# Two transformer blocks on one core: another order of output slabs, a later norm, and a third joint pair of neighbourhood scores

## The chip, the cores and the metric

The kernel runs on one core of one Trainium2 chip. The metric is the device time of one execution in microseconds, and the time of a version is the median over its runs. Engines are named as the profile names them: PE is the matrix engine (PEld its weight loads), DVE the vector engine, ACT the scalar engine, POOL GpSimd and SP the engine that issues the weight transfers.

## What is computed

The input is one sequence of 256 tokens with 1024 features. A first model of two layers is followed by a second of four. The change touches the two layers of the first model only. One of its layers is, cut to what matters:

```
proj = rms_norm(x) @ w_in[l]                 # split into the inputs of four mixers, four heads each
a_out = neighbourhood_attention(...)         # NA: scores + a bias table
b_out = diff_attention(...)                  # two softmaxes per head, subtracted
b_out = rms_norm(b_out, diff_subln[l]) * (1 - lambda_init)     # norm over each head's 64 features
c_out = gqa_attention(...)
d_out = mla_attention(...)
mix = concatenate([a_out, b_out, c_out, d_out]) @ w_o[l]       # 1024 x 1024
x = x + rms_norm(mix, post_mix_norm[l])
x = x + rms_norm(swiglu(rms_norm(x, pre_ffn_norm[l])), post_ffn_norm[l])
```

## The kernel before

All weights stream from memory in units of 128 x 2048 numbers (1 MB). SP loads a unit into one of three `raw` buffers. ACT rounds it to `whi` (L840, `act_hi`), DVE forms the rest `wlo = raw - whi` (L849, `dve_lo`), and each product is done as three matmuls, `hi*hi`, `lo*hi` and `hi*lo`. Every engine has its own instruction stream, written by hand, and runs it in order. Engines meet only in semaphores, on which an instruction waits until a count is reached.

The mixing stage of a layer is a table, `MIX`, of 38 slots (h = 0 to 37). In each slot PE does, in this order: its quarters of weight units; the transposes of one attention head's probabilities (L701, into `pso`), in the slot two after that head's scores; the scores of one head or of a joint pair (L715, into `psu`, and `psy` for the second of a pair); the product with the values of the head whose scores are three slots old (L730, into `psm`); and last, where the table says so, a "turn". Twenty items (heads) are worked on, one begun in each of the slots 12 to 31: four GQA (items 0 to 3), eight halves of the differential heads (4 to 11), four NA (12 to 15) and four MLA (16 to 19). DVE reads an item's scores, adds the table where there is one, and takes the maximum (L810 with a table, L804 without); ACT takes the exponential (L774) and copies the transposed probabilities (L760); DVE divides the finished head into its columns of `rows` (L785 to L796).

The output product runs while the last heads are still being computed. A **turn** m (0 to 7) takes 128 columns (two heads) of `rows`: PE transposes them (L584, two matmuls), ACT casts them into `ahi` (L617), DVE subtracts to get `alo` (L621) and counts the semaphore `m_lo`. A **slab** s (0 to 3) is one weight unit of `w_o` (unit 11 + s of the layer) and consumes the turns 2s and 2s + 1. It has four quarters of six matmuls each (L604, 128x512): two token tiles t, times two halves of its 256 rows. Slots 26 to 29 hold the quarters of slab 0, slots 30 to 33 those of slab 1, slots 34 and 35 two each of slab 2, slots 36 and 37 two each of slab 3. Slab results gather in the four banks of `psy` (tile 0 in banks 0 and 1, tile 1 in banks 2 and 3). The second score of a joint pair also uses bank 2, so slab 0 waits at its third quarter (slot 28) until DVE has read the last joint score.

The columns of `rows` stand in the order GQA, differential, NA, MLA. Turns 2 and 3 are thus those of the differential heads and wait for `mix_ready`, which DVE counts when the norm of these heads is applied. The norm has three steps: `sub_sums` on DVE in slot 26 (L1358 to L1361), a square root on ACT in slot 27 (L1268), `sub_norm` on DVE in slot 27 (L1365 to L1369). The square root and the exponential have different function tables on ACT, so an ACT_TABLE_LOAD stands before the root, another after it (L856), and one more in slot 33, ahead of the root of the next norm.

Of the kernel before, what the change touches and what calls it, by code (L numbers as in the profile page):

```python
# [9 lines left out]
D = 1024  # L10
# [3 lines left out]
HD = 64  # L14
# [31 lines left out]
class Plan:  # L46
# [30 lines left out]
    def value(self, h):  # L77
# [1 line left out]


MIX = Plan([2 if u is None else 4 for u in W_IN1], [3, 3, 2] + [2] * 11 + [1] * 20 + [2] * 4, range(12, 32),
           [17, 19, 28, 29, 30, 31, 33, 35], "00 01 10 02 03 11 12 13",
           [2, 3, 5, 7, 10, 11, 13, 14, 18, 22, 26, 30, 34], 24)
FOX = Plan([4] * 13, [3, 4, 1] + [2] * 30, [9, 10, 11, 12, 13, 14, 15, 16, 17, 18, 19, 20, 23, 24, 25, 26],
           [14, 16, 18, 20, 26, 27, 28, 30], "00 01 10 11 02 12 03 13", None, 23)
SWA = Plan([4] * 6, [2] * 8 + [1] * 15 + [2, 2, 1, 2, 2], range(6, 22), [11, 13, 15, 17, 20, 21, 23, 25],
# [23 lines left out]
def build(nc, wts, ada, ada_b, x_in, c_row, rel_bias, col1, row1, gain_mix, gain_ffn, col2, row2,  # L110
# [4 lines left out]
    with ctx:  # L115
# [18 lines left out]
        rows = sb("rows", [P, NT, D])  # L134
# [449 lines left out]
                last = nc.tensor.transpose(psu[:, bank, t * P:(t + 1) * P], rows[:, t, m * P:(m + 1) * P], ident[:])  # L584
            last.then_inc(m_tr, 1)

        def pe_slab_quarter(pe, l, c, s, part, g, first_t=0):


            t = first_t if part < 2 else 1 - first_t  # L590
            if part == 0:
                pe.wait_ge(lo_done, unit_no(l, c + s) + 1)
            if part < 2:
                pe.wait_ge(m_lo, 8 * g + 2 * s + part + 1)
            k = part_of(c + s)
            toks = slice(t * P, t * P + P)
            if s == 3 and part >= 2:
                chunks = [(0, part - 2), (1, part - 2)]
            else:
                chunks = [(part % 2, 0), (part % 2, 1)]  # L600
            for ff, half in chunks:
                cols = slice(ff * 1024 + half * 512, ff * 1024 + half * 512 + 512)
                for j, (h, b) in enumerate(((ahi, whi[:, k]), (alo, whi[:, k]), (ahi, wlo[:, k]))):
                    last = mm(psy[:, 2 * t + half, :], h[:, (2 * s + ff) % 4, toks], b[:, cols],  # L604
                              start=(s == 0 and ff == 0 and j == 0), stop=(s == 3 and ff == 1 and j == 2),
                              skip_group_check=True)
                if s == 3 and ff == 1 and 2 * t + half < 3:
                    last.then_inc(y_ready, 1)
            if part == 3:
                last.then_inc(unit_mm, 1)  # L610
# [131 lines left out]
        def pe_mix1_turn(pe, l, I0, h):  # L742


            m = MIX.turn.get(h)
            if m is not None:
                if m in (2, 3):
                    pe.wait_ge(mix_ready, l + 1)
                else:
                    pe.wait_ge(o_evac, I0 + (2 * m + 2 if m < 2 else 2 * m + 6))  # L750
                pe_turn(pe, l, m)

        def act_copy(act, I0, items, plan, h):
# [100 lines left out]
        def act_table(func):  # L854

            nc.scalar.activation(spare[:], epsc[:], func)  # L856
# [220 lines left out]
        def na_table(h):  # L1077
            return lambda t: fold(nab[:], NT, 4, SEQ)[:, t, h]
# [11 lines left out]
        def heads1(l):  # L1090
            out, b0 = [], l * 32
            for c in range(2):
                for kv in range(2):
                    ps = slice(64 * kv, 64 * kv + 64)
                    out.append(item(gqT[ps, c * SEQ:(c + 1) * SEQ], gkT[ps, :],
                                    [gv[:, kc * P + kv * HD:kc * P + (kv + 1) * HD] for kc in range(2)],
                                    (2 * c + kv) * HD, pre=(gqa_ready, l + 1), vpre=(bank_free, b0 + 4)))
            for h in range(4):
                for which in range(2):
                    p0, c = 64 * (h % 2) + 32 * which, (h // 2) * SEQ  # L1100
                    ps = slice(p0, p0 + 32)
                    out.append(item(dfq[ps, c:c + SEQ], dfk[ps, c:c + SEQ],
                                    [dfv[:, kc * 256 + h * HD:kc * 256 + (h + 1) * HD] for kc in range(2)],
                                    256 + h * HD, table=distance_table, slope=2.0 ** (-8.0 * (h + 1) / 4), pair=which,
                                    pre=(bank_free, b0 + 6), vpre=(bank_free, b0 + 7)))
            for h in range(4):
                ps, c = slice(64 * (h % 2), 64 * (h % 2) + 64), (h // 2) * SEQ
                out.append(item(naq[ps, c:c + SEQ], nak[ps, c:c + SEQ],
                                [nav[:, kc * 256 + h * HD:kc * 256 + (h + 1) * HD] for kc in range(2)],
                                512 + h * HD, table=na_table(h), tpre=(na_ready, l + 1),  # L1110
                                pre=(bank_free, b0 + 9), vpre=(bank_free, b0 + 10)))
            for h in range(4):
                out.append(item(qcT[0:96, h * SEQ:(h + 1) * SEQ], kcT[0:96, h * SEQ:(h + 1) * SEQ],
                                [mv[:, kc * 256 + h * HD:kc * 256 + (h + 1) * HD] for kc in range(2)],
                                768 + h * HD, pre=(ml_cev, 4 * l + 4), vpre=(ml_evac, l + 1)))
            return out

        def pe_mix1(pe, l):
# [18 lines left out]
            def quarter(j, part):  # L1137
# [3 lines left out]
                if j >= 11:  # L1141
                    if j == 11 and part in (0, 2):
                        pe.wait_ge(bank_free, b0 + 10)
                        if part == 2:
                            pe.wait_ge(max_ready, I0 + sum(MIX.joint))
                        pe.wait_ge(ml_cev, 4 * l + 4)
                    pe_slab_quarter(pe, l, 11, j - 11, part, l)
                    return
                u, at = W_IN1[j], j - (j > C1_SMALL)
                if u == 9:  # L1150
# [44 lines left out]
        def act_mix1(act, l):  # L1195
# [27 lines left out]
            for h in range(MIX.slots):  # L1223
# [38 lines left out]
                if h in (17, 18, 19, 20):  # L1262
                    act.wait_ge(ml_ctr, 4 * l + h - 16)
                    to, h0 = qcT if h < 19 else kcT, (h - 17) % 2 * 2
                    nc.scalar.copy(to[0:96, h0 * SEQ:(h0 + 2) * SEQ], psy[0:96, 3]).then_inc(ml_cev, 1)
                if h == 27:
                    act.wait_ge(sub_sum, l + 1)
                    nc.scalar.activation(gs[:, 1, 0:8], gs[:, 0, 0:8], ACT.Sqrt, bias=epsc[:], scale=1.0 / HD).then_inc(sub_std, 1)  # L1268
                    act_table(ACT.Exp)
                if h in MIX.turn:  # L1270
                    act_turn(act, l, C1_O, MIX.turn[h], l)
                if h == 33:
                    act_table(ACT.Sqrt)
                if j is not None and j < 14:
                    act_hi(act, l, j + SPLIT)

        def dve_mix1(dve, l):
# [71 lines left out]
                nc.vector.tensor_copy(fold(kcat, NT, 4, 96)[:, :, :, 64:96],  # L1349
                                      kr.unsqueeze(2).to_broadcast([P, NT, 4, 32])).then_inc(ml_rope, 1)  # L1350

            dh = rows[:, :, 256:512]
            dh4 = dh.rearrange("p t (h d) -> p t h d", h=4)
            sq, gain64 = qf[:, 0:512], qf[:, 512:512 + HD]

# [14 lines left out]
                                        ALU.mult).then_inc(mix_ready, 1)  # L1370

            for h in range(MIX.slots):
                dve_steps(dve, I0, items, MIX, h, l)
                if h == 3:
                    latent_norm()
# [9 lines left out]
                    head_rope()  # L1385
                if h == 15:
                    latent_rope()
                if h == 26:
                    sub_sums()
                if h == 27:  # L1390
                    sub_norm()
                if h in MIX.lo:
                    dve_lo(dve, l, MIX.lo[h] + SPLIT)
                if h in (16, 20):
# [690 lines left out]
def _weights(a):  # L2085
    units = []
    for l in range(DEPTH1):
# [5 lines left out]
        small[:, :768] = a["mla_w_uq"][l].reshape(2, P, 384).transpose(1, 0, 2).reshape(P, 768)  # L2093
        small[:, 768:1280] = a["mla_w_ukv"][l]
        units += [small if u is None else columns[u] for u in W_IN1]
        w_o = a["w_o"][l].reshape(4, 256, D)[[2, 1, 0, 3]]
        w_o[0] = w_o[0].reshape(4, HD, D)[[0, 2, 1, 3]].reshape(256, D)
        units += _slabs(w_o.reshape(D, D)) + _ffn_units(a["ffn_w_gate_up"][l], a["ffn_w_down"][l])
    seen = {"swa": 0, "gla": 0, "fox": 0}
# [93 lines left out]
```

## Time and profile before

| what | value |
|---|---|
| median of 3 runs (lowest to highest) | 1984.73 us (1979.16 to 1984.73) |
| profiled execution: time / span | 1984.8 us / 1983.0 us |
| PE busy | 1896.8 us, 96% of the span |
| DVE busy / ACT busy | 68% / 50% |
| mixing stage of layer 0, slot 28 begins / slot 34 begins | 126.02 us / 151.28 us |
| mean granted clock of PE | 0.984 |

A row of the timeline gives start, duration, engine, line, operation, the tile written and the tiles read, the number of instructions, and in brackets how long the engine had sat idle before it and what released it. PE's matmuls overlap, so the step from one start to the next is what a matmul costs, not its duration. Layer 1 of the first model repeats layer 0's rows some 344.3 us later (its turn 2 starts at 476.92 us, that of layer 0 at 132.62 us).

### The profile page before, as it was taken

To read this page: it belongs to the slowest core of one execution; us is meant where nothing else is said; L and a number is where in the kernel's file an instruction comes from. 1 tells how busy PE (TensorE), PEld (TensorE's weight loads), DVE (VectorE), ACT (ScalarE), POOL (GpSimd) and SP (SyncE) were. 2 spreads that over 40 slices of the span, in tenths; PEclk is the share of its full clock that TensorE was granted. 3 is DMA by queue.
4 is the path that set the end of the run, shared out by engine and by line. 5 is a ranking of instruction groups with operands and counts; after the bars stand their busy time and mean duration, and the time that the engine had idled before them with its cause. 6 is when DMAs were issued, how large, how long until landed. Compare 5 with 4: busy or idle time off the path is not lost. (4 is left out here: it accounts for less than half of the span.)

```text
span 1983.0 us, 34544 instructions
## 1 busy us (share of the span) xinstructions
PE 1896.8 (96%) x13474; PEld 1741.4 (88%) x13474; DVE 1341.8 (68%) x2132; ACT 996.3 (50%) x1533; POOL 92.8 (5%) x103
## 2 busy tenths in 40 slices
PE   7899999999999999999998999998999999999998
PEld 7788999888899987899978889997889998879997
DVE  4766888665788776688877578886446555665555
ACT  5766333766633366633374463336555334755333
POOL 3102000000000000000000000001800000000000
PEclk9899999999999999999999999999999999999999
DMA  8416988542688842588843258884334554324552
GB/s 290 168 69 196 360 317 317 202 149 77 232 317 310 313 175 80 214 322 313 315 180 118 99 225 324 310 316 175 136 131 165 190 190 169 128 86 170 191 188 87
DMA packets 60210, 412.21 MB, mean 208 GB/s; under 512 B 8576, under 2 KB 8768, under 8 KB 11344
## 3 DMA queue, kind: packets, MB, share of 16 engines
q1 hardware_dynamic: 55584, 401.33, 54.6%
q0 software_dynamic: 4528, 9.56, 1.8%
q8 instruction: 62, 1.02, 0.2%
q14 instruction: 36, 0.29, 0.0%
HBM read 409.71 MB, written 3.16 MB: 208 GB/s over the span
## 5 line engine op out<-in xcount | busy, mean ns | idle before, releaser
L840 ACT CAST whi<-raw 128x2048 fp32r<-128x2048 f32 x282 | 537.9, 1907 | 635.8 <-PE psu L499 424.1
L849 DVE TENSOR_TENSOR wlo<-raw,whi 128x2048 fp32r<-128x2048 f32 (+2 forms) x297 | 651.6, 2195 | 300.2 <-ACT whi L840 299.8
L499 PE MATMUL psu<-hhi,whi 128*128 128x256 f32 x1920 | 537.0, 280 | 0.0
L499 PE MATMUL psu<-hlo,whi 128*128 128x256 f32 x1920 | 536.0, 279 | 0.0
L499 PE MATMUL psu<-hhi,wlo 128*128 128x256 f32 x1920 | 535.8, 279 | 0.0
L499 PEld LDWEIGHTS psu<-hhi,whi 128*128 128x128 f32 x1920 | 360.8, 188 | 3.0
L499 PEld LDWEIGHTS psu<-hlo,whi 128*128 128x128 f32 x1920 | 360.8, 188 | 2.4
L499 PEld LDWEIGHTS psu<-hhi,wlo 128*128 128x128 f32 x1920 | 360.8, 188 | 0.0
L995 DVE CUSTOM_DVE_ANT_0 ada_raw<-ada_raw,cvec 128x1024 f32<-128x1024 f32 x192 | 226.8, 1219 | 0.6 <-DMA ada_raw<-ada 0.6
L655 PE MATMUL psy<-whi,ahi 128*128 128x512 f32 x528 | 210.4, 398 | 1.4 <-DVE alo L1014 1.2
L655 PE MATMUL psy<-wlo,ahi 128*128 128x512 f32 x528 | 208.0, 394 | 0.0
L655 PE MATMUL psy<-whi,alo 128*128 128x512 f32 x528 | 207.5, 393 | 0.0
L558 PE MATMUL psy<-whi,hhi 128*128 128x256 f32 x448 | 133.1, 297 | 1.3 <-DVE wlo L849 1.3
L558 PE MATMUL psy<-whi,hlo 128*128 128x256 f32 x448 | 127.1, 284 | 0.0
L558 PE MATMUL psy<-wlo,hhi 128*128 128x256 f32 x448 | 126.9, 283 | 0.0
L655 PEld LDWEIGHTS psy<-wlo,ahi 128*128 128x128 f32 x528 | 99.1, 188 | 25.3
L655 PEld LDWEIGHTS psy<-whi,ahi 128*128 128x128 f32 x528 | 99.1, 188 | 23.8 <-issue 3.4
L655 PEld LDWEIGHTS psy<-whi,alo 128*128 128x128 f32 x528 | 99.1, 188 | 20.8
L730 PEld LDWEIGHTS psm<-work 128*128 128x128 f32 x608 | 78.2, 196 | 16.0 <-issue 10.7
L558 PEld LDWEIGHTS psy<-whi,hhi 128*128 128x128 f32 x448 | 85.8, 192 | 7.1 <-issue 5.5
L550 PE MATMUL psy<-hhi,whi 128*128 128x256 f32 x288 | 86.2, 299 | 6.0 <-DVE wlo L849 6.0
L774 ACT ACTIVATE work<-work,nmax 128x256 f32<-128x256 f32 (+1 forms) x144 | 66.5, 463 | 46.7 <-DVE nmax L810 46.7
(338 smaller groups left out, 3093.9 us busy)
## 6 DMA issues: line engine op xcount, KB each, us to landing
raw<-wts SPq DMA_DIRECT2D x281, 1024.0 KB, 4.8
ada_raw<-ada SPq DMA_DIRECT2D x96, 1024.0 KB, 4.9
dense_bias<-rel_bias POOLq DMA_DIRECT2D x32, 64.0 KB, 12.3
nab<-dense_bias SPq DMA_DIRECT2D x2, 1024.0 KB, 7.0
ada_raw<-fox_rows POOLq DMA_DIRECT2D x4, 512.0 KB, 7.1
cb<-cst POOLq DMA_DIRECT2D x1, 1408.0 KB, 8.5
cb<-cst SPq DMA_DIRECT2D x1, 1056.0 KB, 12.6
x<-x_in SPq DMA_DIRECT2D x2, 512.0 KB, 4.5
```

The costliest lines, as they stand in the source:

```text
L499: last = mm(psu[:, bank, cc * SEQ:(cc + 1) * SEQ], a[:, cols], h[:, kt, :], start=(kt == 0 and j == 0), stop=(kt == KT - 1 and j == 2))
L550: last = mm(o, a[:, cols], h[:, kt, :], start=(kt == 0 and j == 0), stop=(kt == KT - 1 and j == 2))
L558: last = mm(o, h[:, kt, toks], a[:, kt * width:(kt + 1) * width], start=(kt == 0 and j == 0), stop=(kt == KT - 1 and j == 2))
L655: last = mm(psy[:, 2 * t + half, :], h[:, aslot + ff, toks], b[:, cols], start=False, stop=(last_step and ff == 1 and j == 2), skip_group_ ...
L730: last = mm(psm[:, t * HD:(t + 1) * HD], probT[:, k % 2, at:at + P], it["v"][kc], start=(kc == 0), stop=(kc == 1 or at == P))
L774: last = nc.scalar.activation(prob[:, k % 2, span], src[:, span], ACT.Exp, bias=nmax[:, k % 4, t:t + 1], scale=1.0 if plain else -1.0, acc ...
L840: nc.scalar.copy(whi[:, part_of(c), 0:n], raw[:, slot_of(c), 0:n]).then_inc(hi_done, 1)
L849: last = nc.vector.tensor_tensor(wlo[:, part_of(c), cols], raw[:, slot_of(c), cols], whi[:, part_of(c), cols].bitcast(f32), ALU.subtract)
L995: last = nc.vector.tensor_tensor_reduce(tile, tile, cvec[:], 1.0, 0.0, ALU.mult, ALU.add, ada_part[:, 2 * half + j:2 * half + j + 1])
```

## The change

The columns of `rows` and the row blocks of `w_o` are reordered to GQA, NA, differential, MLA: turns 2 and 3 are now those of the NA heads, turns 4 and 5 those of the differential heads. The turns move from the slots 17, 19, 28, 29, 30, 31, 33, 35 to 17, 19, 29, 31, 32, 33, 34, 35. Slab 1 (unit 12) takes its quarters in another order: first both token tiles with its first 128 rows (turn 2), then both with its second (turn 3). The norm of the differential heads moves to slots 30 (`sub_sums`), 31 (root) and 32 (`sub_norm`, ahead of the other DVE steps of the slot), and two table loads per layer go. The scores of the NA heads 2 and 3 (items 14 and 15) are issued as one joint pair in slot 26.

```diff
 MIX = Plan([2 if u is None else 4 for u in W_IN1], [3, 3, 2] + [2] * 11 + [1] * 20 + [2] * 4, range(12, 32),
-           [17, 19, 28, 29, 30, 31, 33, 35], "00 01 10 02 03 11 12 13",
-           [2, 3, 5, 7, 10, 11, 13, 14, 18, 22, 26, 30, 34], 24)
+           [17, 19, 29, 31, 32, 33, 34, 35], "00 01 10 02 03 11 12 13",
+           [2, 3, 5, 7, 10, 11, 13, 14, 18, 22, 26, 30, 34], 26)
...
-        def pe_slab_quarter(pe, l, c, s, part, g, first_t=0):
+        def pe_slab_quarter(pe, l, c, s, part, g, first_t=0, by_tile=True):
-            t = first_t if part < 2 else 1 - first_t
+            t, half_rows = (part // 2, part % 2) if by_tile else (part % 2, part // 2)
+            t = t if first_t == 0 else 1 - t
             if part == 0:
                 pe.wait_ge(lo_done, unit_no(l, c + s) + 1)
-            if part < 2:
-                pe.wait_ge(m_lo, 8 * g + 2 * s + part + 1)
+            if part == half_rows or not by_tile:
+                pe.wait_ge(m_lo, 8 * g + 2 * s + half_rows + 1)
...
-                chunks = [(part % 2, 0), (part % 2, 1)]
+                chunks = [(half_rows, 0), (half_rows, 1)]
...
-                if m in (2, 3):
+                if m in (4, 5):
                     pe.wait_ge(mix_ready, l + 1)
                 else:
-                    pe.wait_ge(o_evac, I0 + (2 * m + 2 if m < 2 else 2 * m + 6))
+                    pe.wait_ge(o_evac, I0 + {0: 2, 1: 4, 2: 14, 3: 16, 6: 18, 7: 20}[m])
...
-                    pe_slab_quarter(pe, l, 11, j - 11, part, l)
+                    pe_slab_quarter(pe, l, 11, j - 11, part, l, 0, j != 12)
...
-                if h == 27:
+                if h == 31:
                     act.wait_ge(sub_sum, l + 1)
                     nc.scalar.activation(gs[:, 1, 0:8], gs[:, 0, 0:8], ACT.Sqrt, bias=epsc[:], scale=1.0 / HD).then_inc(sub_std, 1)
-                    act_table(ACT.Exp)
                 if h in MIX.turn:
                     act_turn(act, l, C1_O, MIX.turn[h], l)
-                if h == 33:
-                    act_table(ACT.Sqrt)
...
             for h in range(MIX.slots):
+                if h == 32:
+                    sub_norm()
                 dve_steps(dve, I0, items, MIX, h, l)
...
-                if h == 26:
+                if h == 30:
                     sub_sums()
-                if h == 27:
-                    sub_norm()
...
-        w_o = a["w_o"][l].reshape(4, 256, D)[[2, 1, 0, 3]]
+        w_o = a["w_o"][l].reshape(4, 256, D)[[2, 0, 1, 3]]
```

PE's stream of layer 0, from the end of slot 28 into slot 29, before the change (`psm<-work` is the product with the values, `psu<-ident,rows` the turn, `psy<-whi,ahi` the first matmul of a quarter):

```order
L730 MATMUL psm<-work 128x64 [waits bank_free,o_evac,pt_ready]
L730 MATMUL psm<-work 128x64 x3
L584 MATMUL psu<-ident,rows 128x128 [waits m_lo,mix_ready]
L584 MATMUL psu<-ident,rows 128x128
L604 MATMUL psy<-whi,ahi 128x512
```

and PE's stream from the end of slot 31 into slot 32, first before the change, then with it (where L604 has become L605):

```order
L730 MATMUL psm<-work 128x64 [waits ml_evac,o_evac,pt_ready]
L730 MATMUL psm<-work 128x64 x3
L584 MATMUL psu<-ident,rows 128x128 [waits m_lo,o_evac]
L584 MATMUL psu<-ident,rows 128x128
L604 MATMUL psy<-whi,ahi 128x512
```

```order
L731 MATMUL psm<-work 128x64 [waits ml_evac,o_evac,pt_ready]
L731 MATMUL psm<-work 128x64 x3
L584 MATMUL psu<-ident,rows 128x128 [waits m_lo,o_evac]
L584 MATMUL psu<-ident,rows 128x128
L605 MATMUL psy<-whi,ahi 128x512 [waits m_lo]
```

In slot 28 the turn that waited for `mix_ready` is gone; in slot 31 the turn is now turn 3 and not turn 5, and the quarter right behind it waits for that turn's `m_lo`, which it did not before. The same pair, a turn and right behind it a quarter that waits for it, now also stands at the border of slots 29 and 30, with turn 2.

ACT's stream of slot 31 and the start of slot 32, before the change and with it (`work,psum_<-psu,nmax` is the exponential of the last item, `ahi<-psu` the cast of a turn, `work<-pso` the copy of transposed probabilities):

```order
L774 ACTIVATE work,psum_<-psu,nmax 128x256 [waits t_done,max_ready]
L774 ACTIVATE work,psum_<-psu,nmax 128x256
L617 CAST ahi<-psu 128x256 [waits unit_mm,m_tr]
L760 COPY work<-pso 128x512 [waits o_done,t_done] x2
L617 CAST ahi<-psu 128x256 [waits unit_mm,m_tr]
```

```order
L775 ACTIVATE work,psum_<-psu,nmax 128x256 [waits t_done,max_ready]
L775 ACTIVATE work,psum_<-psu,nmax 128x256
L1269 ACT_TABLE_LOAD
L1269 ACTIVATE gs<-gs,epsc 128x8 [waits sub_sum]
L618 CAST ahi<-psu 128x256 [waits m_tr]
L761 COPY work<-pso 128x512 [waits o_done,t_done]
```

The table load and the root now stand between the last exponential and the cast of turn 3.

## Rows read from the trace of the kernel before

**Rows 1.** The page, busy time of PE: time, share of the span, instructions.

```profile
PE 1896.8 (96%) x13474; PEld 1741.4 (88%) x13474; DVE 1341.8 (68%) x2132; ACT 996.3 (50%) x1533; POOL 92.8 (5%) x103
```

**Rows 2.** Waits of PE, whole span: us in total, times, longest.

```profile
PE psy L626 <- DVE rows L913: 28.3, 12, 8.4
...
PE psu L584 <- DVE rows L1369: 5.1, 2, 2.5
```

**Rows 3.** Timeline of PE, layer 0, slots 27 to 34 (L604 starts a slot).

```profile
122.02 0.48 PE L604 MATMUL psy<-whi,ahi 128*128 128x512 f32 x1
...
126.02 0.48 PE L604 MATMUL psy<-whi,ahi 128*128 128x512 f32 x1
...
128.12 1.13 PE L715 MATMUL psu<-work 96*128 96x256 f32 x4
...
132.62 0.69 PE L584 MATMUL psu<-ident,rows 128*128 128x128 f32 x2 [2.54 <-DVE rows L1369]
132.96 0.78 PE L604 MATMUL psy<-whi,ahi 128*128 128x512 f32 x1
...
138.09 0.48 PE L604 MATMUL psy<-whi,ahi 128*128 128x512 f32 x1
...
141.88 0.47 PE L604 MATMUL psy<-whi,ahi 128*128 128x512 f32 x1
...
145.50 0.39 PE L584 MATMUL psu<-ident,rows 128*128 128x128 f32 x2
145.65 0.48 PE L604 MATMUL psy<-whi,ahi 128*128 128x512 f32 x1
...
148.38 0.48 PE L604 MATMUL psy<-whi,ahi 128*128 128x512 f32 x1
...
151.28 0.48 PE L604 MATMUL psy<-whi,ahi 128*128 128x512 f32 x1
```

**Rows 4.** Timeline of PE, slot 24: two matmuls of a joint pair.

```profile
113.85 0.38 PE L715 MATMUL psu<-work 64*128 64x256 f32 x1
113.86 0.38 PE L715 MATMUL psy<-work 64*128 64x256 f32 x1
```

**Rows 5.** Timeline of DVE, slots 26 and 27: norm sums, split, maximum of item 15.

```profile
123.55 0.69 DVE L1358 TENSOR_TENSOR work<-rows 128x512 f32<-128x512 f32 x1
...
125.09 2.28 DVE L849 TENSOR_TENSOR wlo<-raw,whi 128x2048 fp32r<-128x2048 f32 x1
...
127.98 0.08 DVE L810 DVE_READ_ACCUMULATOR2_ANT nmax<- 128x1 f32 x1
```

**Rows 6.** Timeline of ACT and DVE, slot 30: the cast and subtraction of turn 4.

```profile
142.74 0.37 ACT L617 CAST ahi<-psu 128x256 fp32r<-128x256 f32 x1
...
143.14 0.42 DVE L621 TENSOR_TENSOR alo<-psu,ahi 128x256 fp32r<-128x256 f32 x1 [0.67 <-ACT ahi L617]
```

**Rows 7.** Timeline of DVE and ACT, slots 30 and 31: division, split, exponential, cast.

```profile
142.18 0.29 DVE L792 TENSOR_TENSOR rows<-psm,rsum 128x128 f32<-128x128 f32 x1
...
143.48 2.28 DVE L849 TENSOR_TENSOR wlo<-raw,whi 128x2048 fp32r<-128x2048 f32 x1
...
147.22 0.20 ACT L774 ACTIVATION_READ_ACCUMULATOR work<-psu,nmax 128x1 f32 x1
147.31 0.37 ACT L617 CAST ahi<-psu 128x256 fp32r<-128x256 f32 x1
```

**Rows 8.** Timeline of ACT, slot 27: the two table loads around the root.

```profile
129.21 1.28 ACT L1268 ACT_TABLE_LOAD   x1
...
130.82 1.28 ACT L856 ACT_TABLE_LOAD   x1
```

**Rows 9.** Windows: us, busy times, PEclk the granted clock, DMA share, GB/s.

```profile
132.60:134.60 2.00, 1.98 (x6) 1.69 (x7) 1.01 (x4) 1.47 (x6) 0.00 (x0) 0.50 0.00 0
...
751.00:754.00 3.00, 2.91 (x25) 2.61 (x26) 1.38 (x7) 1.49 (x6) 0.00 (x0) 1.00 0.61 254
```

**Rows 10.** Timeline of PE in the second model: a shorter idle time.

```profile
751.09 0.34 PE L715 MATMUL psu<-work 64*128 64x128 f32 x1 [1.88 <-ACT work L1637]
```

More of the change, by code:

```diff
@@ L1103, in heads1 @@
                                     [dfv[:, kc * 256 + h * HD:kc * 256 + (h + 1) * HD] for kc in range(2)],
-                                    256 + h * HD, table=distance_table, slope=2.0 ** (-8.0 * (h + 1) / 4), pair=which,
+                                    512 + h * HD, table=distance_table, slope=2.0 ** (-8.0 * (h + 1) / 4), pair=which,
                                     pre=(bank_free, b0 + 6), vpre=(bank_free, b0 + 7)))
@@ L1109, in heads1 @@
                                 [nav[:, kc * 256 + h * HD:kc * 256 + (h + 1) * HD] for kc in range(2)],
-                                512 + h * HD, table=na_table(h), tpre=(na_ready, l + 1),
+                                256 + h * HD, table=na_table(h), tpre=(na_ready, l + 1),
                                 pre=(bank_free, b0 + 9), vpre=(bank_free, b0 + 10)))
@@ L1350, in latent_rope @@
                                       kr.unsqueeze(2).to_broadcast([P, NT, 4, 32])).then_inc(ml_rope, 1)
-            dh = rows[:, :, 256:512]
+            dh = rows[:, :, 512:768]
             dh4 = dh.rearrange("p t (h d) -> p t h d", h=4)
```

## The prediction

> **What bounds the kernel now.** I read the page first: PE is busy for 96% of the span [rows 1]. So only what makes PE idle, slows its clock or adds to its stream can move the time. The waits of PE name what is left: 28.3 us before the norms between stages, and, in the stage that is changed, 5.1 us in two waits of the turn's transpose (L584) for the last step of the differential norm (L1369) [rows 2]. Then the timeline of the mixing stage. Its slots are best read by their first L604. An ordinary slot with scores and a turn takes 141.88 - 138.09 = 3.79 us, and slot 32, with neither, 148.38 - 145.65 = 2.73 us [rows 3]. The exception is slot 28. It begins at 126.02, its turn cannot start until 132.62 after 2.54 us of idle time, and slot 29 then takes 138.09 - 132.96 = 5.13 us instead of 3.79 [rows 3], because PE had been idle: the granted clock reads 0.50, which is 1.2 of 2.4 GHz [rows 9]. Since PE has no other gap of note until the stage ends, and the feed-forward stage behind it keeps PE full, I take every microsecond of a slot to reach the end of the span.
>
> The norm was late because its root stands behind a table load, and that behind item 15's exponential; the load with its root takes 130.82 - 129.21 = 1.61 us [rows 8].
>
> **What goes.** Slots 28 and 29 took 138.09 - 126.02 = 12.07 us [rows 3]. With the change no turn stands in slot 28, and slot 29's turn 2 is that of NA heads divided by slot 28. A turn's own issue costs PE 145.65 - 145.50 = 0.15 us [rows 3]. So they need 3.79 - 0.15 + 3.79 = 7.43 us: a gain of **4.64 us** per layer. What is late next is looked for below.
>
> **The joint pair.** The second score of a pair is free on PE: the matmuls into `psu` and `psy` start 0.01 us apart [rows 4]. Slot 27, without scores, would so be over after about 2.73 us, at 122.02 + 2.73 = 124.75. But slot 28 opens with slab 0's third quarter, which writes bank 2 of `psy` and must now wait for item 15's maximum. Before, that maximum ended at 127.98 + 0.08 = 128.06, and the next scores went right behind it at 128.12 [rows 3, 5]. It stood behind `sub_sums`, 125.09 - 123.55 = 1.54 us [rows 5], which leave slot 26; the split of 2.28 us stays ahead of it. So slot 28 begins at 128.12 - 1.54 = 126.58 instead of 126.02: a loss of **0.56 us**. The joint pair wins nothing; PE waits 126.58 - 124.75 = 1.8 us for what it saved.
>
> **The wait at slot 30.** Turn 2 now ends slot 29, and the first quarter of slot 30 needs its halves at once. Before there was a slot between. Behind the turn stand ACT's exponential and cast and DVE's subtraction. In slot 30 of before the same chain ended at 143.14 + 0.42 = 143.56 [rows 6], with the next slot begun at 141.88 [rows 3], or 1.73 us later with 0.05 us for the semaphore. Slot 30 loses a turn in exchange (0.15). Net **+1.58 us**.
>
> **The wait at slot 32.** Turn 3 ends slot 31, and slab 1's third quarter needs it at once. I count from the first L604 of slot 30, 138.09 before. DVE ended the division at 142.18 + 0.29 = 142.47 and began the split at 143.48, as it had turn 4 to subtract between [rows 7]. Now `sub_sums` stand there: the split begins 0.09 + 1.54 us behind the division, at 144.10, 0.62 us later. Behind the split are queued item 19's maximum and, on ACT, its exponential, whose last read ended at 147.22 + 0.20 = 147.42 [rows 7]; that becomes 148.04. Then come the table load and the root, 1.61 us [rows 8]; the cast of turn 3 starts at 149.67, its subtraction 143.14 - 142.74 = 0.40 us behind that [rows 6] and ends at 150.49; PE goes on at 150.54, or 12.45 us after slot 30 began. PE itself is ready after slot 30 without its turn (3.64) and slot 31 (145.65 - 141.88 = 3.77 [rows 3]), at 7.41. The wait is **5.04 us**. It is twice the wait that was removed, and it must cost the clock too: 2.54 us of idle time cost slot 29 5.13 - 3.79 = 1.34 us [rows 3], which I charge again. The wait is bounded below by what the chain takes without the norm's parts, 5.04 - 0.62 - 1.61 = 2.8 us, and the clock's price by 0.
>
> Slot 32 also takes a turn it did not have (+0.15), slot 33 keeps one, slot 34 gets one (+0.15). Turn 4 needs `sub_norm`, three DVE steps behind turn 3's subtraction; they lie beside slot 32, which lasts over 2.73 us. Turn 5 is needed at slot 34's second quarter, 1.4 us behind the turn, against 1.3 us of cast and subtraction with ACT and DVE free: no wait, by little. No DMA moves its place in SP's queue; the units are split in the same slots.
>
> **Table loads.** Two of three per layer go. The load before the root stays on the path (it is in the 5.04 us); the second stood beside PE's wait, the third, in slot 33, beside PE's work. I cost the two that go at nothing beyond what is in the 4.64 us. The Trainium skill, "ScalarE: Activation LUTs", section "What ACT_TABLE_LOAD costs", puts every switch at 2.66 us, load and drain; the rows show 1.28 us for the load and 0.01 us until the root, no drain of its own. Its advice to group functions by table speaks for this change, and by its figure four switches would be worth 4 x 2.66 = 10.6 us, if they lay on the path, and the time 1974 us.
>
> **Sum per layer:** -4.64 + 0.56 + 1.58 + 5.04 + 1.34 + 0.15 + 0.15 = **+4.18 us**, for two layers +8.4 us. The profiled execution took 1984.8 us, the median is 1984.73; I predict 1984.8 + 8.4 = 1993.2 us.
>
> **Rivals.**
>
> *The clock falls at the short waits too* (1.8 us before slot 28, 1.7 before slot 30). An idle time of 1.88 us elsewhere [rows 10] left the clock at 1.00 [rows 9], but here several waits come close together. Each would cost up to 1.34 us: 4 x 1.34 = 5.4 us, 1998.6 us. Chance 0.15.
>
> *The waits are there but smaller:* slot 32's at its lower bound of 2.8 us takes off 2.2 us per layer and leaves 8.4 - 4.5 = 3.9 us, 1988.7 us; or the clock is not lost, 1990.5 us. Against it: rows of DVE and ACT before give every step. Chance 0.16.
>
> *Faster: the turn's latency is not seen by PE.* If the halves of turns 2 and 3 were there when slots 30 and 32 open, 1.73 + 5.04 + 1.34 us would go: 4.18 - 8.11 = -3.93 per layer, 1976.9 us. It decides once the two waits together (with the clock) are under 8.11 - 4.18 - 3.0 = 0.9 us, since 3.0 us per layer must be won. For it: the wait that is removed is the largest in the stage. Against it: the chain is four steps on two engines and the quarter follows the turn directly. Chance 0.06.
>
> *Faster: ACT's time is the path.* Then four loads with their dummy activation (1.28 + 0.2) go, 5.9 us, 1978.9 us. By the Trainium skill's grouping rule this is the expected effect. Against it: PE, not ACT, is full. Chance 0.04.
>
> My forecast has the rest, 0.59, with its own range of 1990 to 1996.
>
> **How the numbers follow.** 0.3% of the time is 6 us, about what a measurement of this kernel can tell from no change; its three runs alone span 0.28%. Slower by over 0.3% means above 1990.7 us: the clock rival and most of the forecast (a run in the lower group, near 1979, would pull it under), 0.67. Within 0.3%: the rest of the forecast, the smaller waits and a part of the faster ones, 0.25. Faster by over 0.3%: 0.08. The range runs from 1985 us, below the smaller waits, to 1999.5 us, above the clock rival.
>
> **What would show it.** Right: no wait of L584 for L1367; slot 28 begins near 126.6; the first L605 of slot 30 waits some 1.5 us and that of slot 32 some 5 us, both for the subtraction L622; the granted clock is near 0.5 behind the latter; ACT shows table load, root and cast in a row under it; slot 34 begins near 155.3 instead of 151.28. Wrong: no idle time of PE at slot 32, or a clock that stays at 1.00 behind it, or a feed-forward stage whose PE was not full and takes up the delay.

## The result, and the profile after

| | before | changed |
|---|---|---|
| median of 15 runs each | 1982.13 us | 1993.38 us |
| lowest to highest | 1978.96 to 1985.45 us | 1984.40 to 1998.80 us |
| ratio to before (95% interval) | | 1.0058 (1.0046 to 1.0069) |

The change makes the kernel slower by 0.58%, 11.3 us by the medians. Forecast were 1993.2 us and +8.4 us against a profiled execution of 1984.8 us; with more runs the median of before came down to 1982.13 us, so the loss is 2.9 us larger than the forecast one. That the absolute time agrees to 0.2 us is luck: a base that was 2.7 us too high made up for most of a loss forecast too small.

The page of the changed kernel answers to [rows 1]: PE's busy time has grown by 2.2 us, and its span by 11.7 us, to 1994.7 us.

```profile
PE 1899.0 (95%) x13474; PEld 1744.0 (87%) x13474; DVE 1341.6 (67%) x2132; ACT 991.5 (50%) x1525; POOL 91.6 (5%) x103
```

The view of PE's waits, as in [rows 2] (us in total, times, longest):

```profile
PE psy L627 <- DVE rows L914: 28.3, 12, 8.5
PE psy L605 <- DVE alo L622: 13.2, 6, 4.7
...
PE psy L605 <- issue: 5.4, 5, 1.5
```

The waits of the turn for the norm are gone. In their place the slabs' matmuls (L605) wait for the subtraction of a turn's halves (L622), 13.2 us in all. The row "issue" holds the two waits of 1.50 us ahead of slot 28 among its five (before had 2.5 us in three): the last read of item 15's maximum on DVE ended at 127.05 us in layer 0, slot 28 began at 127.16, and the view names nobody for it.

PE's timeline in layer 0, slots 27 to 34, against [rows 3]:

```profile
122.74 0.48 PE L605 MATMUL psy<-whi,ahi 128*128 128x512 f32 x1
...
127.16 0.55 PE L605 MATMUL psy<-whi,ahi 128*128 128x512 f32 x1 [1.50 <-issue]
...
132.34 0.49 PE L605 MATMUL psy<-whi,ahi 128*128 128x512 f32 x1
...
137.94 0.47 PE L605 MATMUL psy<-whi,ahi 128*128 128x512 f32 x1 [1.59 <-DVE alo L622]
...
141.53 0.48 PE L605 MATMUL psy<-whi,ahi 128*128 128x512 f32 x1
...
145.15 0.39 PE L584 MATMUL psu<-ident,rows 128*128 128x128 f32 x2
150.25 0.79 PE L605 MATMUL psy<-whi,ahi 128*128 128x512 f32 x1 [4.71 <-DVE alo L622]
...
155.24 0.48 PE L605 MATMUL psy<-whi,ahi 128*128 128x512 f32 x1
...
158.16 0.48 PE L605 MATMUL psy<-whi,ahi 128*128 128x512 f32 x1
```

The steps between these starts are the slots. Turn 3 is issued at 145.15, and the quarter behind it begins 5.1 us later. Who holds it stands in the timeline of DVE and ACT, slots 30 to 32, against [rows 7] and [rows 8]:

```profile
143.93 2.28 DVE L850 TENSOR_TENSOR wlo<-raw,whi 128x2048 fp32r<-128x2048 f32 x1
...
146.12 0.68 DVE L805 TENSOR_REDUCE nmax<-psu 128x2 f32<-128x512 f32 x1
...
147.66 0.20 ACT L775 ACTIVATION_READ_ACCUMULATOR work<-psu,nmax 128x1 f32 x1
147.88 1.28 ACT L1269 ACT_TABLE_LOAD   x1
149.18 0.30 ACT L1269 ACTIVATE gs<-gs,epsc 128x8 f32<-128x8 f32 x1
149.38 0.35 ACT L618 CAST ahi<-psu 128x256 fp32r<-128x256 f32 x1
149.77 0.42 DVE L622 TENSOR_TENSOR alo<-psu,ahi 128x256 fp32r<-128x256 f32 x1 [2.52 <-ACT ahi L618]
```

It is the forecast chain, link by link: split, maximum, exponential, table load, root, cast, subtraction. The windows of the changed kernel show what the clock did behind three of the waits, as pairs of layer 0 and layer 1 (PEclk is the third number from the right): behind slot 28's, slot 30's and slot 32's.

```profile
127.20:129.20 2.00, 2.00 (x5) 1.54 (x6) 0.29 (x1) 0.99 (x4) 0.00 (x0) 0.55 0.96 266
476.20:478.20 2.00, 2.00 (x11) 1.68 (x12) 0.29 (x1) 1.01 (x4) 0.00 (x0) 1.00 0.75 246
138.00:140.00 2.00, 2.00 (x11) 1.68 (x12) 0.00 (x0) 1.14 (x1) 0.00 (x0) 1.00 0.04 8
485.40:487.40 2.00, 2.00 (x6) 1.55 (x7) 0.00 (x0) 1.18 (x1) 0.00 (x0) 0.60 0.00 0
150.30:152.30 2.00, 2.00 (x5) 1.61 (x6) 1.39 (x3) 0.00 (x0) 0.00 (x0) 0.50 1.06 446
499.30:501.30 2.00, 2.00 (x5) 1.63 (x6) 1.43 (x3) 0.00 (x0) 0.00 (x0) 0.50 1.01 426
```

The granted clock was at its lower level, 0.50, behind the long wait in both layers. Behind the two short waits it fell once in each layer, and not behind the same one.

### The profile page after: what moved, and what is told of

Read it like the earlier page. It is cut to its first block and busy times, and to the rows that moved or that the text cites. A ratio compares the mean times of both kernels' runs of the same rounds, so it can differ in the third digit from the quotient of the medians.

```text
span 1994.7 us, 34534 instructions
## 1 busy us (share of the span) xinstructions
PE 1899.0 (95%) x13474; PEld 1744.0 (87%) x13474; DVE 1341.6 (67%) x2132; ACT 991.5 (50%) x1525; POOL 91.6 (5%) x103
## 5 line engine op out<-in xcount | busy, mean ns | idle before, releaser
L656 PE MATMUL psy<-whi,ahi 128*128 128x512 f32 x528 | 210.4, 399 | 1.4 <-DVE alo L1015 1.3
L605 PE MATMUL psy<-whi,ahi 128*128 128x512 f32 x192 | 83.1, 433 | 18.6 <-DVE alo L622 13.2
```

The lines of the kernel that those rows point to most:

```text
L656: last = mm(psy[:, 2 * t + half, :], h[:, aslot + ff, toks], b[:, cols], start=False, stop=(last_step and ff == 1 and j == 2), skip_group_ ...
```

## The experiments

The theory: PE pays the latency of a turn wherever the quarter that needs it follows directly, and that latency includes whatever stands on DVE and ACT ahead of the cast and the subtraction. The rivals: the joint pair, the new slab order or the later norm cost by themselves, or the table loads are what counts. Executions of one kernel differ by some 6 to 14 us, so beside the medians I read one quantity from each profile, which is one execution: the time from the first matmul of slot 26 to that of slot 34. Before, it is 151.28 - 118.05 = 33.23 us in layer 0 and 33.32 us in layer 1.

| kernel | median (n), us | ratio to before (95%) | slots 26 to 33, layer 0 / 1, us |
|---|---|---|---|
| changed | 1993.38 (15) | 1.0058 (1.0046 to 1.0069) | 39.41 / 39.02 |
| cast_first | 1990.24 (8) | 1.0040 (1.0025 to 1.0055) | 36.97 / 35.93 |
| filler | 1993.43 (6) | 1.0048 (1.0034 to 1.0063) | 37.31 / 37.38 |
| no_joint | 1992.21 (6) | 1.0050 (1.0036 to 1.0065) | 38.21 / 36.69 |
| joint_only | 1980.41 (12) | 0.9991 (0.9980 to 1.0002) | 32.42 / 32.49 |
| turns_28_30 | 1991.36 (8) | 1.0036 (1.0023 to 1.0048) | 36.30 / 35.60 |
| turns_split33 | 1983.70 (12) | 1.0001 (0.9991 to 1.0012) | 33.63 / 32.07 |
| turns_split33_joint | 1980.56 (12) | 0.9989 (0.9976 to 1.0002) | 31.21 / 32.85 |
| split33_cast | 1988.04 (12) | 1.0021 (1.0009 to 1.0033) | 35.70 / 34.16 |
| root_early | 1973.89 (6) | 0.9955 (0.9938 to 0.9972) | 29.30 / 29.33 |
| root_early_joint | 1971.48 (7) | 0.9955 (0.9938 to 0.9972) | 28.65 / 28.65 |

The medians of before beside them were 1982.63 us for cast_first to joint_only, 1983.22 us for turns_28_30 to split33_cast and 1980.50 us for the last two; the times expected below count from 1982 to 1983 us for before, so about 1 us of what the second group is above its expectations is the base. The slots go with the ratios: over all eleven kernels, the difference of the two layers' slots from before's 66.55 us lies within 2 us of what the ratio says. For the changed kernel it is 78.43 - 66.55 = 11.9 us against 11.5, for root_early 58.63 - 66.55 = -7.9 us against -8.9.

### cast_first: ACT's cast of turn 3 ahead of the root

```diff
+                if h in MIX.turn:
+                    act_turn(act, l, C1_O, MIX.turn[h], l)
                 if h == 31:
                     act.wait_ge(sub_sum, l + 1)
                     nc.scalar.activation(gs[:, 1, 0:8], gs[:, 0, 0:8], ACT.Sqrt, bias=epsc[:], scale=1.0 / HD).then_inc(sub_std, 1)
-                if h in MIX.turn:
-                    act_turn(act, l, C1_O, MIX.turn[h], l)
```

> The changed kernel with ACT's order in slot 31 turned round: the cast of turn 3 first, then the table load and the root. Theory (the latency of turn 3 is what PE waits for in slot 32, and the table load with its root stands in it): PE's idle time there falls by 1.6 us, from 4.7 to about 3.1 us in each layer, sub_norm still ends before turn 4 needs it, and the time falls by 3.2 us, from 1993.4 to about 1990 us (1988 if the clock drops for a shorter stretch behind the shorter wait). Rival (DVE's late maximum alone holds the chain, and the load lies beside it): no change, 1993.4 us. Rival (the norm itself is now late): PE waits for mix_ready at turn 4 and the time does not fall.

PE's wait at slot 32 in layers 0 and 1, from the timeline of this kernel, and the windows behind it:

```profile
145.60 0.80 PE L605 MATMUL psy<-whi,ahi 128*128 128x512 f32 x1 [3.09 <-DVE alo L622]
...
494.83 0.50 PE L605 MATMUL psy<-whi,ahi 128*128 128x512 f32 x1 [3.09 <-DVE alo L622]
```

```profile
145.60:147.60 2.00, 2.00 (x5) 1.61 (x6) 0.79 (x2) 1.09 (x2) 0.00 (x0) 0.50 1.00 422
494.80:496.80 2.00, 1.97 (x11) 1.65 (x12) 0.77 (x2) 1.12 (x2) 0.00 (x0) 1.00 1.02 430
```

The wait fell by 4.71 - 3.09 = 1.62 us, as the load and its root last. The median is 3.1 us lower, as expected; the intervals of the two ratios overlap, so it is the wait that shows the effect. The one table load that stood on the path cost its full length, and sub_norm was not late for turn 4. The same idle time of 3.09 us dropped the clock in layer 0 and left it at 1.00 in layer 1.

### filler: matmuls of zeros in the wait

```diff
                 pe_mix1_turn(pe, l, I0, h)
+                if h == 31:
+                    pe.wait_ge(pt_ready, I0 + 18)
+                    for _ in range(20):
+                        mm(fold(pso[:], 4, P), zeros[:], zeros[:].unsqueeze(1).to_broadcast([P, 4, P]), start=True, stop=True)
```

> The changed kernel with 20 matmuls of zeros, 128x512 each, issued by PE into pso behind turn 3 in slot 31, where it otherwise sits idle; pso holds nothing then. Nothing else changes, and the wait for turn 3's halves ends when it did. Theory (idle time drops the clock, and this is part of the price): the fillers take about 20 x 0.23 = 4.6 us of the 5 us wait, the granted clock stays at 1.00, slot 32 takes 2.9 us instead of 5.0 and 4.6, and the time falls by about 4 us, from 1993.4 to 1989.5 us. Rival (the clock falls whatever PE does there): slot 32 keeps its 4.6 to 5.0 us and the time is 1993.4 us. Rival (the fillers overrun the wait): up to 1 us per layer slower than the first case.

The wait for `pt_ready` holds the fillers back until `pso` has been read. The timeline of PE, layer 0, with the start of slot 33 as its last row, and the granted clock during the fillers and behind them:

```profile
142.83 4.48 PE L1198 MATMUL pso<-zeros 128*128 128x512 bf16 x20
...
147.70 0.50 PE L605 MATMUL psy<-whi,ahi 128*128 128x512 f32 x1 [0.39 <-DVE alo L622]
...
150.63 0.48 PE L605 MATMUL psy<-whi,ahi 128*128 128x512 f32 x1
```

```profile
143.00:147.00 4.00, 4.00 (x20) 1.76 (x18) 1.63 (x4) 2.67 (x7) 0.00 (x0) 1.00 0.61 190
147.70:149.70 2.00, 2.00 (x12) 1.68 (x12) 1.44 (x3) 0.00 (x0) 0.00 (x0) 1.00 1.01 426
```

Slot 31 kept its length (8.71 us, against 8.72), since the fillers shorten nothing of the chain. Slot 32 took 2.93 us and in layer 1 2.92 us, where the changed kernel took 4.99 and 4.57. That is the clock's price behind the long wait: 2.06 and 1.65 us, and keeping PE busy saved it. The whole execution did not show it: I expected 1989.5 us, the median is the changed kernel's, and the intervals of the ratios, 2 us apart, overlap. In the profiled execution the two layers' slots gained 3.7 us, while stages whose code is the same in both lost 4.6 us: by PE's timeline the attention stages of the second model's first three layers took 104.4, 155.2 and 141.8 us, against 103.9, 153.2 and 139.6 us in the changed kernel. Two waits of PE make 3.3 us of the 4.6: in the third of these stages it waited 4.2 us for ACT ahead of L702, where the eleven other profiles have 1.6 to 2.7, and in the second 3.3 us for DVE ahead of L1551, where they have 1.7 or 1.8. Whether the fillers bring this about, and whether the 3.7 us would stand out over more runs, is open.

### no_joint and joint_only: the pair, taken away and by itself

Both change one number, the last argument of `MIX`: 26 becomes 24 in the changed kernel, 24 becomes 26 in the kernel before.

> The changed kernel without the third joint pair (items 14 and 15 scored singly again). Theory (the pair only trades 1.06 us of PE work for a wait on item 15's maximum): slot 28 begins 0.4 us earlier, without idle time ahead of it, so in a layer where the clock fell behind that wait another 1.5 us are won; but the wait at slot 30 may then be the one that drops the clock. Between 0.8 and 3.8 us faster than 1993.4 us, about 1991 us. Rival (the joint pair is what makes the change slow): back to within 3 us of before, below 1985 us. Rival (the pair is worth its matmuls): 2 us slower, 1995.5 us.

> The kernel before with the third joint pair alone. Theory: slot 28 can begin only behind item 15's maximum, which stands behind sub_sums and the split, at 128.1 instead of 126.0 us in layer 0, but the turn at the end of that slot waited for the norm until 132.6 anyway, so the later start is covered; if the clock falls ahead of slot 28 instead of behind it, that moves and does not add. Within 1.5 us of before, 1981 to 1983.5 us. Rival (the pair costs what slot 28 is late): 2 x 2.1 = 4.2 us slower, 1986.3 us. Rival (the pair wins its matmuls): 2 x 1.06 = 2.1 us faster, 1980 us.

Without the pair, slot 28 followed slot 27 without a wait (3.99 us for slot 27, not 4.42) and kept the clock in both layers; slot 30's wait was unchanged and dropped it in layer 0 alone. Slots 26 to 33 gained 1.20 and 2.33 us, and the median fell by 1.2 us, far from the 1985 us at which the pair would have been the cause: it was not what made the change slow.

By itself the pair did slightly better than I expected: 1980.41 us is close to the 1980 us of the rival by which it wins its matmuls. The slots show another reason. PE's timeline of joint_only, starts of slots 28 and 29:

```profile
127.02 0.47 PE L604 MATMUL psy<-whi,ahi 128*128 128x512 f32 x1 [3.21 <-issue]
...
132.38 0.48 PE L604 MATMUL psy<-whi,ahi 128*128 128x512 f32 x1
```

Slot 27 is 6.14 us long instead of 4.00 and slot 28 5.36 instead of 6.94, so the two take 0.56 us more; the wait for the norm is covered, and the drop of the clock stands in slot 28 instead of slot 29, which takes 3.77 us instead of 5.13. I had said that the drop moves and does not add; it moved to a place where part of it was covered by the norm's lateness. Slots 26 to 33 gained 0.8 us per layer; the ratio's interval still touches 1.

### turns_28_30: a slot between the turn and its quarter

```diff
-           [17, 19, 29, 31, 32, 33, 34, 35], "00 01 10 02 03 11 12 13",
-           [2, 3, 5, 7, 10, 11, 13, 14, 18, 22, 26, 30, 34], 26)
+           [17, 19, 28, 30, 32, 33, 34, 35], "00 01 10 02 03 11 12 13",
+           [2, 3, 5, 7, 10, 11, 13, 14, 18, 22, 26, 30, 34], 24)
```

> The changed kernel without the third joint pair and with turns 2 and 3 one slot earlier, in slots 28 and 30: a slot now lies between each turn and the quarter that needs it, and each turn instead waits some 0.65 us for its last head's division. Theory (PE pays for the turn's latency wherever nothing lies between, and a wait that goes uncovers the next): no wait for halves at slots 30 and 32; but the subtraction of turn 3 now stands ahead of sub_sums and the split on DVE, so the last maximum, the exponential, the root and sub_norm end about 14.6 us after slot 30 began, and turn 4 at the end of slot 32, ready at 11.5, waits 3.1 us for mix_ready, with a clock drop behind it. Slots 26 to 33 take about 35.2 us instead of 39.2 (33.2 before): about 1986.5 us. Rival (the new slab order or the norm costs by itself): stays above 1990 us. Rival (nothing else is late): slots 26 to 33 take 30.7 us, 1977 us.

PE's timeline of this kernel: the starts of slots 31 and 32, turn 4 at the end of slot 32, and the start of slot 33.

```profile
138.65 0.48 PE L605 MATMUL psy<-whi,ahi 128*128 128x512 f32 x1
...
142.25 0.48 PE L605 MATMUL psy<-whi,ahi 128*128 128x512 f32 x1
...
148.77 0.69 PE L584 MATMUL psu<-ident,rows 128*128 128x128 f32 x2 [2.88 <-DVE rows L1367]
149.11 0.78 PE L605 MATMUL psy<-whi,ahi 128*128 128x512 f32 x1
```

The waits for halves are gone (slot 31, 8.72 us in the changed kernel, takes 142.25 - 138.65 = 3.60), and each of the two turns waited 0.6 us for a division. The next late thing was the norm, as expected: turn 4 waited 2.88 us for L1367. The slots took 36.30 and 35.60 us where I expected 35.2, with a costlier drop of the clock in slot 33. The time, 1991.4 us, is 5 us above what I expected of it, more than the slots' 1.5 us in all and the 1 us of the base account for. It is also above the 1990 us that I had set for the rival "the new slab order or the norm costs by itself", and for the norm that rival is right: with the waits for halves gone, its lateness at turn 4 is the largest wait left in these slots. For the new slab order no slot shows a cost (slots 29 and 31 take 3.60 us each), but no run has it alone.

### turns_split33, turns_split33_joint, split33_cast: the split off the chain

The first adds to turns_28_30 that unit 14 is split in slot 33 (30 becomes 33 in the list of splits). The second also sets the pair and splits unit 13 in slot 28 (26 becomes 28). The third is the changed kernel with the split in slot 33 and the diff of cast_first; its turns are where the change put them.

> As turns_28_30, and the split of unit 14 on DVE moves from slot 30 to slot 33, so that it no longer stands ahead of the last maximum. Theory: the maximum is then read as soon as the scores are there, the root ends 1.9 us earlier, turn 4 waits 1.8 us instead of 3.1 us and mostly without a clock drop; slots 26 to 33 take about 31.9 us, 1.4 us less than before the change: about 1979.5 us. Rival (the split's transfer or unit 14 is then late): a new wait of PE on the split at slot 36, slower than turns_28_30. Rival (it was the table load that held the norm): no change against turns_28_30.

> As turns_split33, with the third joint pair back and the split of unit 13 moved from slot 26 to slot 28, so that item 15's maximum stands right behind the transposes of slot 27. Theory (a joint pair is worth its matmuls once its maximum isn't late): slot 27 takes 2.9 us instead of 4.0 and slot 28 begins without a wait of note; slots 26 to 33 take about 30.9 us: about 1977.5 us. Rival (the pair is worth nothing even so, as in the changed kernel): 1979.5 us or more.

> The changed kernel with only DVE's and ACT's order changed: the split of unit 14 in slot 33, and the cast of turn 3 ahead of the table load and the root. The turns stay where the change put them. Theory (the wait at slot 32 is a sum of a plain turn's latency, the split and sums ahead of the last maximum, and the load with its root): it falls from 4.7 us to about 1.6 us of idle time, and the clock mostly stays; slots 26 to 33 take about 34.3 us instead of 39.2: about 1983.5 us, near before. Rival (what is left is more than the turn's latency): the idle time stays above 2.5 us and the time above 1987 us.

One row from each timeline, layer 0: turn 4 in turns_split33, slot 28 in turns_split33_joint, slot 32 in split33_cast.

```profile
148.14 0.65 PE L584 MATMUL psu<-ident,rows 128*128 128x128 f32 x2 [1.65 <-DVE rows L1367]
```

```profile
125.13 0.47 PE L605 MATMUL psy<-whi,ahi 128*128 128x512 f32 x1 [0.21 <-issue]
```

```profile
147.93 0.50 PE L605 MATMUL psy<-whi,ahi 128*128 128x512 f32 x1 [1.49 <-DVE alo L622]
```

Turn 4 waited 1.65 us instead of 2.88, by the split's move alone. The clock dropped behind it in layer 0 and not in layer 1, which makes the 1.6 us between the layers' slots. The time came out 4 us above the expected one, level with before, and that of turns_split33_joint 3 us above. With its maximum no longer behind a split, the pair was worth 3.99 - 3.14 = 0.85 us of slot 27 per layer. By the time alone this is not shown: 1980.56 us lies above the 1979.5 us that I had set for "the pair is worth nothing", and the intervals of the two kernels overlap. In split33_cast what was left of the wait at slot 32 is 1.49 us of idle time, the bare latency of a turn and the same as slot 30's 1.59. The long wait is thus taken apart: 4.71 = 1.49 + 1.62 (load and root) + 1.60 (the split, which the sums ahead of it had made later). Its time, 1988.0 us, is above the expected 1983.5 us and above the rival's 1987, though its idle time is not the rival's. The clock dropped behind the remaining 1.49 us too, in both layers: slot 32 takes 4.53 us in each, 1.6 more than filler's. The slots, 69.86 us in all against 68.6 expected, and the base make 2.4 of the 4.5 us; the rest is not explained.

### root_early and root_early_joint: the removed wait, removed otherwise

Here the kernel before is changed in one place: ACT's root and its two table loads move from behind item 15's exponential in slot 27 to ahead of it, where ACT sat waiting for DVE.

```diff
                 act_copy(act, I0, items, MIX, h)
+                if h == 27:
+                    act.wait_ge(sub_sum, l + 1)
+                    nc.scalar.activation(gs[:, 1, 0:8], gs[:, 0, 0:8], ACT.Sqrt, bias=epsc[:], scale=1.0 / HD).then_inc(sub_std, 1)
+                    act_table(ACT.Exp)
                 act_exp(act, I0, items, MIX, h)
...
-                if h == 27:
-                    act.wait_ge(sub_sum, l + 1)
-                    nc.scalar.activation(gs[:, 1, 0:8], gs[:, 0, 0:8], ACT.Sqrt, bias=epsc[:], scale=1.0 / HD).then_inc(sub_std, 1)
-                    act_table(ACT.Exp)
```

The second also has the pair (26) and splits unit 13 in slot 28.

> The kernel before, with its turns, slabs and pairs, and one move on ACT: the root of the differential norm with its two table loads goes ahead of item 15's exponential in slot 27, where ACT sat idle 3.4 us for DVE's maximum (124.7 to 128.1 us in layer 0). Theory (the removed wait was the norm's lateness and can be removed without making anything else late): the root ends at about 126.4 us, sub_norm at 130.3 us, and PE's turn 2, ready at 130.1, waits 0.3 us instead of 2.5 us, with no clock drop in slot 29; no wait at slots 30 and 32. Slots 26 to 33 take 29.0 us instead of 33.3: about 8.5 us faster, 1974 us. Rival (the exponential is late by the second load): T15 in slot 29 waits up to 0.5 us more, 1975 us. Rival (the gain of 4.6 us per layer in my sum was not there): above 1979 us.

> As root_early, with the third joint pair and the split of unit 13 moved from slot 26 to slot 28. Theory (the pair is worth its 1.06 us of PE less what item 15's maximum is then late behind sub_sums, some 0.8 us in slot 27): 0.3 us per layer faster than root_early, and its wait of 0.3 us for the norm goes too: about 1973 us. Rival (the late split of unit 13 now delays item 17's maximum and so slot 30): 1 us per layer slower than root_early, 1976 us.

The timeline of root_early, ACT and PE, slots 27 to 29:

```profile
123.43 1.28 ACT L1230 ACT_TABLE_LOAD   x1
...
124.72 0.30 ACT L1230 ACTIVATE gs<-gs,epsc 128x8 f32<-128x8 f32 x1
125.04 1.28 ACT L856 ACT_TABLE_LOAD   x1
...
126.77 0.51 ACT L774 ACTIVATE work<-work,nmax 128x256 f32<-128x256 f32 x1 [0.23 <-DVE nmax L810]
...
128.87 0.44 PE L584 MATMUL psu<-ident,rows 128*128 128x128 f32 x2
129.07 0.48 PE L604 MATMUL psy<-whi,ahi 128*128 128x512 f32 x1
...
132.84 0.48 PE L604 MATMUL psy<-whi,ahi 128*128 128x512 f32 x1
```

Both loads lie in time in which ACT had nothing to do: the exponential still waits 0.23 us for its maximum. The turn starts without a bracket, and slot 29 takes 3.77 us. The time is 1973.9 us, as expected, 6.6 us below before by the medians and 0.45% by the ratio, with all three table loads still there. The pair adds no difference that the ratios show (0.9955 both), though its slots are 0.7 us per layer shorter. The gain is in slot 28 (3.77 us instead of 4.38) and not in slot 27 (3.93 instead of 3.99): the maximum of item 15, no longer behind a split, makes nothing late in slot 28. These two versions beat both kernels.

## Why the prediction was right, and where a size was off

The range, the sign and the mechanism held. By its steps, as slots of the changed kernel's two layers:

| step | forecast, us | layer 0 / layer 1, us |
|---|---|---|
| slot 27 with its wait for item 15's maximum | 4.56 | 4.42 / 4.42 |
| slot 28, no turn, clock at full rate | 3.64 | 5.18 / 3.59 |
| slot 29 and the wait for turn 2's halves | 3.79 + 1.73 = 5.52 | 5.60 / 5.61 |
| slot 30, no turn | 3.64 | 3.59 / 5.19 |
| slot 31 and the wait for turn 3's halves | 3.77 + 5.04 = 8.81 | 8.72 / 8.72 |
| slot 32, turn 4, behind the drop of the clock | 2.73 + 0.15 + 1.34 = 4.22 | 4.99 / 4.57 |
| slot 33 | 2.90 | 2.92 / 2.92 |

**The gain of 4.64 us for the removed wait** was there. root_early, which removes that wait and nothing else, shortened the slots by 3.93 and 3.99 us. It keeps the turn in slot 28 (0.15 us), and slot 28 is still 4.38 - 3.79 = 0.6 us longer than an ordinary one; together these are the 4.64. The 0.6 us are not all the norm's: in root_early the weight loads of PE waited both for item 15's maximum and for the norm.

```profile
126.79 0.73 PEld L715 LDWEIGHTS psu<-work 96*128 96x128 f32 x4 [0.25 <-DVE nmax L810]
...
128.87 0.20 PEld L584 LDWEIGHTS psu<-ident,rows 128*128 128x128 f32 x2 [0.25 <-DVE rows L1369]
```

It is the new waits that outweighed the gain.

**The joint pair wins nothing** held in the changed kernel: PE waited 1.50 us for the maximum where I said 1.8. The cause I named, the split ahead of that maximum, is borne out by turns_split33_joint, where the split is out of the way and the pair is worth 0.85 us.

**The two waits for halves** are right to 0.1 us each (the start of the cast should be 148.04 + 1.61 = 149.65, not 149.67), and their composition was shown by taking them apart (cast_first, split33_cast). The "lower bound of 2.8 us" was too high for what can be had by reordering: moving the split as well left 1.49 us of idle time. It was the rival's figure, not the forecast's: the prediction left the split on the chain.

**Table loads off the path at nothing**: borne out for the two that went. root_early keeps all three, two of them moved, and its slots have their ordinary lengths but for the 0.6 us above. The third load ran beside slot 34 (at 151.95 us before); that slot now takes 162.02 - 158.16 = 3.86 us where it took 154.99 - 151.28 = 3.71, which is the turn that it gained, and PE's waits before the norms are 28.3 us in both kernels. The load that stayed cost 1.62 us, with the root, because it was moved onto the path. By the Trainium skill's "ScalarE: Activation LUTs", section "What ACT_TABLE_LOAD costs", a switch takes 2.66 us with its drain; no run here shows more than the 1.28 us of the load, 1.62 us with the root. The rival that ACT's time is the path fell.

**The term that was mis-sized is the clock.** I charged 1.34 us per layer, behind the wait at slot 32 only. There it cost 2.06 and 1.65 us (filler against the changed kernel). The 1.34 us were read off slot 29 of layer 0 alone; of the same drop in layer 1 before, slot 29 takes 482.46 - 477.11 = 5.35 us, or 1.57 more than 3.78:

```profile
476.92 0.44 PE L584 MATMUL psu<-ident,rows 128*128 128x128 f32 x2 [2.54 <-DVE rows L1369]
477.11 0.64 PE L604 MATMUL psy<-whi,ahi 128*128 128x512 f32 x1
...
482.46 0.48 PE L604 MATMUL psy<-whi,ahi 128*128 128x512 f32 x1
```

In layer 0 a part of the drop had fallen on the turn itself, which took 132.96 - 132.62 = 0.34 us instead of 0.15. And the clock dropped behind one short wait in each layer as well, for 1.54 us in layer 0 (5.18 - 3.64) and 1.55 in layer 1 (5.19 - 3.64). That is the rival "the clock falls at the short waits too", half of it: I had given it a chance of 0.15 as all or nothing, where each such wait has a chance of its own. These terms sum to 2.06 + 1.65 + 1.54 + 1.55 - 2 x 1.34 = 4.1 us; the slots of both layers came to 78.43 us where the steps of the forecast add up to 74.5, and the other steps together are off by 0.2 us.

## What to carry to other kernels

When a producer with a latency over several engines is moved later, look at what now follows it directly on the engine that is the bound: a slot between a turn and its use had hidden 1.7 us, and what else is queued on the helping engines adds to that wait (here a table load with its root its full 1.62 us, a split of 2.28 us 1.60). Saving table loads on an engine that waits was worth nothing here; putting them into its idle time, as root_early does, removed the same stall without a new one. And an idle time of the matrix engine is better charged with a chance of a drop of its clock than with a fixed price: behind waits of 1.5 to 1.7 us here, and of 3.09 us, it sometimes fell and sometimes did not.

## What the runs showed that I had not expected

The clock's answer to the same idle time is not the same from one layer to the next. Over the profiles of the changed kernel, cast_first, filler, no_joint and split33_cast, the idle times of 1.50 us before slot 28 were followed by a lengthened slot (5.17 or 5.18 us instead of 3.6) in 2 of 8 cases, and those of 1.59 us before slot 30 in 5 of 10; the 1.49 us before slot 32 of split33_cast in both layers, and the 1.65 us before turn 4 of turns_split33 and turns_split33_joint in 2 of 4. The waits of 2.54, 2.88 and 3.21 us (before, turns_28_30, joint_only) and of 4.7 us (changed, no_joint) were followed by a drop in all ten cases. Of two idle times of 3.09 us in one execution (cast_first), one was followed by a granted clock of 0.50 and the other by 1.00. Where it fell it cost some 1.3 to 2.6 us. This may be a part of the 6 to 14 us by which executions of one kernel differ, but no run shows it: the changed kernel, with six waits in place of two, ranged over 14.4 us and before over 6.5 us, yet root_early, in whose profile the clock did not drop in these slots, ranged over 7.4 us in 6 runs, and turns_split33_joint over 13.5 us in 12.
